# Value times gate and its remainder moved from GpSimd to VectorE in the feed-forward stage

## The chip, the core and the metric

The kernel runs on one core of a Trainium2 chip. A core has five engines with a queue each: TensorE (PE, matrix products), VectorE (DVE), ScalarE (ACT), GpSimd (POOL) and SyncE (SP), which here issues DMAs. Each queue runs in order; between engines an instruction waits for semaphores. The metric is the device time of one execution in microseconds (us).

## The reference, cut to what matters

Two transformer blocks over 256 tokens of width 1024, everything in float32. Only the feed-forward part of the first block is touched:

```
h2 = modulate(rms_norm(x, g_ffn), sh_f, sc_f)
u = einsum('bsd,df->bsf', h2, w_up)                  # 1024 -> 2 * 2816
u = causal_depthwise_conv(u, w_conv, b_conv)         # 3 taps along the tokens
u_val, u_gate = split(u, 2)
y = einsum('bsf,fd->bsd', gelu(u_gate) * u_val, w_down)   # 2816 -> 1024
x = x + gt_f * y
```

The rows `mod = silu(c) @ w_mod + b_mod` of the second block (shifts, scales and gates) are computed on VectorE in the gaps of the same stage.

## The kernel before, in words

Every product of float32 matrices is made of three TensorE products of rounded parts: `a` is `hi + lo`, `hi` is `a` rounded to float32r and `lo` the remainder, and the result is hi*hi + hi*lo + lo*hi (`triple`, L1344). Activations lie with features on the partitions and 256 tokens along the free dimension. Weights arrive in chunks of 128x2048 floats (1 MB) through four raw buffers, loaded by SP in the order `stream_order` lays down. For each chunk ScalarE casts the high part (`split` on ScalarE, L371, `w_hi`) and VectorE subtracts it (`split` on VectorE, L865, `w_lo`, called the weight remainder below); there are three slots of each, and a slot is free when TensorE has used the chunk that is three earlier (`lin_done`).

The feed-forward stage has 11 rounds, c = 0 to 10. A round has three chunks: 256 value columns, 256 gate columns and the 256 rows of `w_down` that take them in; 48 matmuls each. TensorE's order is up value(c), up gate(c), down(c-1) up to down(7); the last three down-projections stand behind round 10. Rounds 2 to 8 and 9 also carry a modulation chunk: it needs no TensorE, VectorE multiplies and sums it in four partial sums (`mod`, L832), which use a slot of `w_lo` as their waste output. In a round, by the functions' names:

- ScalarE `value_part(c)`: cast of a chunk (not in rounds 1 and 10, where `product_hi` has done it), then the first tap of the value filter out of PSUM into `cv` (`conv_first`, L560). It waits for TensorE's value block and for `g_lo_done` of round c-1, since `cv` is still read until then.
- VectorE `conv_taps(0, ...)`: the other two taps (L1034, L1039), in place; then a weight remainder.
- ScalarE `gate_part(c)` and VectorE `conv_taps(1, ...)`: the same for the gate in `cg`; then a weight remainder, in rounds 1 to 8 and 10.
- ScalarE `product_hi(c)`: gelu of `cg` (L588); behind the product, the cast of `cv` to `g_hi` (L596).
- GpSimd `product(c)`: `cv = cv * cg` behind gelu (L336), and behind the cast `g_lo = cv - g_hi` (L339).
- TensorE `down(c)` waits for `g_lo_done` and for its weights.

`cv`, `cg` and the pair `g_hi`/`g_lo` are one buffer each (round 9's pair lies in `h_hi`/`h_lo`). VectorE also has, ahead of round 10's value taps and behind its gate taps, two pieces of a norm for the next stage (`norm`, L899 and L905), into the first of which the weight remainder `ffn_up(10) + 2` is set (`chunk=`). After the last round VectorE reads the result out of PSUM bank by bank (L1074), and TensorE sums squares of it (L1601) between the last blocks of the last down-projection.

## Time and profile before

| | |
|---|---|
| median of 3 runs | 795.64 us (795.53 to 795.8) |
| the profiled execution | 795.57 us |
| its span | 793.8 us, granted clock 0.99 |
| PE busy | 751.9 us (95%) |
| DVE busy | 649.1 us (82%) |
| ACT busy | 387.9 us (49%) |
| POOL busy | 46.2 us (6%), 31 instructions |
| feed-forward stage | about 241 to 435 us |

The times in the rows further down count from the span's start. A matmul is shown with its whole latency (0.28 us), while the next one starts 0.12 us later, so a wait of TensorE under 0.2 us does not appear as idle time; the distance between two starts shows it. On VectorE and ScalarE too an instruction may start a little before the last one has ended, and the distance from start to start is what one takes of the queue. In a row of the timeline the bracket behind it is the idle time ahead of it and what ended it.

### The profile page before, as it was taken

Reading aid. Unit: us, or ns where it says so; the run is one execution under the profiler, and the core shown is the slowest. Engines: PE = TensorE matmul, PEld = TensorE weight load, DVE = VectorE, ACT = ScalarE, POOL = GpSimd, SP = SyncE. Lnnn points to the kernel's source line nnn. Section 1 sums busy time; section 2 is a strip of 40 time slices with the busy share of each in tenths; the row PEclk is TensorE's granted clock in tenths of the full one; section 3 lists DMA queues with packets and bytes.
Section 4 is the critical chain, followed back from the end, with each engine's and each line's share of the span. In section 5 each row is a group of like instructions: output and inputs, shape, how many; then the busy total and the mean of one; then the engine's idle time right before and its main releaser. Section 6 shows DMA issues by size and latency. Waiting matters only on the chain.

```text
span 793.8 us, 13124 instructions
## 1 busy us (share of the span) xinstructions
PE 751.9 (95%) x5479; PEld 697.9 (88%) x5480; DVE 649.1 (82%) x1001; ACT 387.9 (49%) x521; POOL 46.2 (6%) x31
## 2 busy tenths in 40 slices
PE   0499999999999999999999999999999999999996
PEld 0399999999999999999999998888778899999995
DVE  3988767995897799999898779999989956987752
ACT  2355645557547654544547532322463335365742
POOL 0000000000000422223222000000000000000000
PEclk9799999999999999999999999999999999999998
DMA  9999998765563557766645241313106643563101
GB/s 347 417 352 365 368 348 311 264 223 198 206 240 136 208 212 251 273 246 247 258 175 197 91 176 53 107 55 104 54 0 235 224 148 118 225 231 118 54 1 54
DMA packets 26086, 156.58 MB, mean 197 GB/s; under 512 B 2691, under 2 KB 7084, under 8 KB 7852
## 3 DMA queue, kind: packets, MB, share of 16 engines
q1 hardware_dynamic: 21392, 148.91, 50.5%
q10 hardware_dynamic: 4636, 6.85, 2.6%
q8 instruction: 43, 0.70, 0.3%
q14 instruction: 15, 0.12, 0.0%
HBM read 154.68 MB, written 1.06 MB: 196 GB/s over the span
## 4 chain that ended last, share of the span: by engine, by line
PE 84%; DVE 9%; ACT 3%; issue 1%; ACTq 1%; POOL 1%; DVEq 0%
PE psum L1344 71%; DVE w_lo L832 4%; PE psum L1379 2%; DVE w_lo L865 2%; PE psum L1636 1%; PE psum L1810 1%; PE psum L1786 1%; ACT w_hi L371 1%; PE psum L1798 1%; PE psum L1622 1%; PE psum L1486 1%; DVE arena L1034 1%; DVE arena L1039 0%; PE psum L1601 0%; PE psum L1471 0%
## 5 line engine op out<-in xcount | busy, mean ns | idle before, releaser
L1344 PE MATMUL psum<-h_hi,w_hi 128*128 128x256 f32 (+1 forms) x1312 | 397.2, 303 | 10.2 <-DVE h_lo L905 9.2
L1344 PE MATMUL psum<-h_lo,w_hi 128*128 128x256 f32 (+1 forms) x1312 | 392.1, 299 | 0.0
L1344 PE MATMUL psum<-h_hi,w_lo 128*128 128x256 f32 (+1 forms) x1312 | 392.1, 299 | 0.0
L1344 PEld LDWEIGHTS psum<-h_hi,w_hi 128*128 128x128 f32 x1312 | 251.1, 191 | 21.8 <-issue 11.6
L1344 PEld LDWEIGHTS psum<-h_lo,w_hi 128*128 128x128 f32 x1312 | 251.5, 192 | 7.8 <-issue 0.2
L1344 PEld LDWEIGHTS psum<-h_hi,w_lo 128*128 128x128 f32 x1312 | 251.3, 192 | 7.4
L865 DVE TENSOR_TENSOR w_lo<-raw,w_hi 128x2048 fp32r<-128x2048 f32 x93 | 212.7, 2288 | 50.2 <-ACT w_hi L371 49.4
L371 ACT CAST w_hi<-raw 128x2048 fp32r<-128x2048 f32 x93 | 176.9, 1905 | 20.6 <-DMA raw<-in_w 16.3
L832 DVE SCALAR_TENSOR_TENSOR w_lo<-raw,cond 128x1024 fp32r<-128x1024 f32 x88 | 119.5, 1395 | 8.3 <-PE psum L1344 7.5
L832 DVE SCALAR_TENSOR_TENSOR w_lo<-raw,arena 128x1024 fp32r<-128x1024 f32 x48 | 56.8, 1221 | 0.8
L336 POOL TENSOR_TENSOR arena<-arena 128x512 f32<-128x512 f32 x11 | 26.1, 2370 | 372.9 <-ACT arena L588 372.9
L1344 PE MATMUL psum<-g_hi,w_hi 128*128 128x256 f32 x160 | 45.7, 286 | 1.7 <-POOL g_lo L339 0.9
L1090 DVE SCALAR_TENSOR_TENSOR arena<-att,vec,arena 128x256 f32<-128x256 f32 x116 | 47.0, 479 | 0.1
L1344 PE MATMUL psum<-g_lo,w_hi 128*128 128x256 f32 x160 | 45.3, 283 | 0.0
L1344 PE MATMUL psum<-g_hi,w_lo 128*128 128x256 f32 x160 | 45.3, 283 | 0.0
L560 ACT ACTIVATE arena<-psum,vec 128x256 f32<-128x256 f32 x44 | 22.4, 561 | 37.3 <-PE psum L1344 34.2
L388 ACT ACTIVATE att<-xs 128x256 f32<-128x256 f32 x32 | 12.4, 412 | 46.5 <-DVE xs L1197 24.1
L1344 PEld LDWEIGHTS psum<-g_hi,w_hi 128*128 128x128 f32 x160 | 30.6, 191 | 2.1 <-issue 1.1
L405 ACT ACTIVATE h_hi<-att,modv 128x256 fp32r<-128x256 f32 x48 | 23.0, 506 | 16.4 <-DVE att L899 16.4
L1344 PEld LDWEIGHTS psum<-g_lo,w_hi 128*128 128x128 f32 x160 | 30.6, 191 | 0.0
L1344 PEld LDWEIGHTS psum<-g_hi,w_lo 128*128 128x128 f32 x160 | 30.6, 191 | 0.0
L899 DVE SCALAR_TENSOR_TENSOR att<-xs,coef,rstd 128x256 f32<-128x256 f32 x40 | 20.4, 534 | 11.3 <-ACT rstd L398 11.1
(214 smaller groups left out, 783.7 us busy)
## 6 DMA issues: line engine op xcount, KB each, us to landing
raw<-in_w SPq DMA_DIRECT2D x141, 1024.0 KB, 4.9
xs<-in_xs ACTq DMA_DIRECT2D x2, 1024.0 KB, 12.0
consts<-diff ACTq DMA_DIRECT2D x8, 128.0 KB, 5.5
cond<-in_cond ACTq DMA_DIRECT2D x1, 1024.0 KB, 6.4
out<-xs SPq DMA_DIRECT2D x4, 256.0 KB, 2.4
arena<-in_cond ACTq DMA_DIRECT2D x1, 512.0 KB, 6.8
consts<-in_c ACTq DMA_DIRECT2D x1, 512.0 KB, 3.4
arena<-in_c ACTq DMA_DIRECT2D x1, 448.0 KB, 3.2
```

The costliest lines, as they stand in the source:

```text
L336: nc.gpsimd.tensor_tensor(cv, cv, cg, ALU.mult).then_inc(sem("ffn_mult"), 1)
L371: nc.scalar.copy(w_hi[:, slot, :], raw[:, rslot, :]).then_inc(sem("hi_done"), 1)
L388: nc.scalar.activation(square_tmp(name)[:, k, :], xs[:, k, s * T:(s + 1) * T], ACT.Square).then_inc(sem(f"sq_{name}"), 1)
L405: nc.scalar.activation(h_hi[:, k, s * T:(s + 1) * T], norm_tmp[:, k, :], ACT.Identity, bias=shift_col(sh, k, v), scale=1.0).then_inc(sem(" ...
L560: nc.scalar.activation(dst[:, t, :], (src or bank[which])[:, t * T:(t + 1) * T], ACT.Identity, bias=col("b_conv", tile), scale=col("w_conv ...
L832: last = nc.vector.scalar_tensor_tensor(w_lo[:, slot, D * t:D * (t + 1)], raw[:, rslot, D * t:D * (t + 1)], 1.0, c, ALU.mult, ALU.mult, ac ...
L865: nc.vector.tensor_tensor(w_lo[:, slot, :], raw[:, rslot, :], w_hi[:, slot, :].bitcast(F32), ALU.subtract).then_inc(sem("lo_done"), 1)
L899: nc.vector.scalar_tensor_tensor(norm_tmp[:, k, :], xs[:, k, s * T:(s + 1) * T], coef[:, at + k:at + k + 1], rstd_of, ALU.mult, ALU.mult). ...
L1034: me.mark(nc.vector.scalar_tensor_tensor(dst[:, t, 1:T], src[:, t * T:(t + 1) * T - 1], col("w_conv", 44 + tile), dst[:, t, 1:T], ALU.mult ...
L1090: nc.vector.scalar_tensor_tensor(out, src, weight, acc, ALU.mult, ALU.add).then_inc(sem("conv_tap"), 1)
L1344: last = mm(out, w[a], x[b], start=start and n == 0, stop=stop and n == 2, skip_group_check=skip)
L1379: last = mm(bank[2 + s][:, s * T:(s + 1) * T], ones, square_tmp(name)[:, k, :], start=(k == 0), stop=(k == KT - 1))
```

## The change

GpSimd's `product` is gone; GpSimd keeps two groups of memsets. VectorE gets the same two operations as two functions, `product(c)` and `product_lo(c)`, and they are called at fixed places: the product at the end of round c, behind the weight remainder that follows the gate's taps; its remainder at the start of round c+1, behind the modulation chunk and the weight remainder there. Around rounds 9 and 10 they are set in by hand: the remainder of round 9 inside the first piece of the norm, the product and remainder of round 10 inside the last. ScalarE's and TensorE's instructions and the order of the DMAs are the same; they wait for the same semaphores.

```
-            def product(c):
-                pool.wait_ge(sem("gelu_done"), c + 1)
-                pool.wait_ge(sem("value_conv"), c + 1)
-                nc.gpsimd.tensor_tensor(cv, cv, cg, ALU.mult).then_inc(sem("ffn_mult"), 1)
-                pool.wait_ge(sem("g_hi_done"), c + 1)
-                hi, lo = ffn_g(c)
-                nc.gpsimd.tensor_tensor(lo, cv, hi.bitcast(F32), ALU.subtract).then_inc(sem("g_lo_done"), 1)
-            for c in range(FF_STEPS):
-                product(c)
...
-            def norm(name, coefs_before, rstd_of=None, ks=range(KT), chunk=None):
+            def norm(name, coefs_before, rstd_of=None, ks=range(KT), between=None):
...
-                    if i == len(ks) and chunk is not None:
-                        split(chunk)
+                    if i == len(ks) and between:
+                        between()
...
+            def product(c):
+                dve.wait_ge(sem("gelu_done"), c + 1)
+                dve.wait_ge(sem("value_conv"), c + 1)
+                nc.vector.tensor_tensor(cv, cv, cg, ALU.mult).then_inc(sem("ffn_mult"), 1)
+            def product_lo(c):
+                dve.wait_ge(sem("g_hi_done"), c + 1)
+                hi, lo = ffn_g(c)
+                nc.vector.tensor_tensor(lo, cv, hi.bitcast(F32), ALU.subtract).then_inc(sem("g_lo_done"), 1)
+            def last_split_of_values():
+                split(ffn_up(FF_STEPS - 1) + 2)
+                product_lo(FF_STEPS - 2)
+            def last_product():
+                product(FF_STEPS - 1)
+                split(ffn_down(FF_STEPS - 3) + 2)
+                product_lo(FF_STEPS - 1)
...
-                    norm("even_ctx", 4, ks=(4, 5), chunk=ffn_up(c) + 2)
+                    norm("even_ctx", 4, ks=(4, 5), between=last_split_of_values)
                 else:
                     split(ffn_up(c) + 2)
+                    if c:
+                        product_lo(c - 1)
                 conv_taps(0, cv, c, bank[2] if c == 0 else None)
                 split(ffn_up(c) + 3)
                 conv_taps(1, cg, c)
-                if 0 < c < FF_STEPS - 2 or c == FF_STEPS - 1:
-                    split(ffn_down(c - 1 if c < FF_STEPS - 2 else c - 2) + 2)
-            norm("even_ctx", 4, ks=(6, 7))
+                if 0 < c < FF_STEPS - 2:
+                    split(ffn_down(c - 1) + 2)
+                if c < FF_STEPS - 1:
+                    product(c)
+            norm("even_ctx", 4, ks=(6, 7), between=last_product)
```

VectorE's queue from the end of round 1 into round 2, before: weight remainder, the four partial sums of the modulation chunk, weight remainder, value taps.

```order
L865 TENSOR_TENSOR w_lo<-raw,w_hi 128x2048 [waits hi_done]
L832 SCALAR_TENSOR_TENSOR w_lo,modv<-raw,cond 128x1024 [waits mod_done,lin_done,arrived1]
L832 SCALAR_TENSOR_TENSOR w_lo,modv<-raw,cond 128x1024
L832 SCALAR_TENSOR_TENSOR w_lo,modv<-raw,cond 128x1024 [waits dve_steps]
L832 SCALAR_TENSOR_TENSOR w_lo,modv<-raw,cond 128x1024
L865 TENSOR_TENSOR w_lo<-raw,w_hi 128x2048 [waits hi_done,mod_done]
L1034 SCALAR_TENSOR_TENSOR arena<-psum,vec,arena 128x255 [waits tap2]
```

The same place now (the file's lines have moved by 11 there: L854 is the weight remainder, L821 the partial sums, L1023 the taps).

```order
L854 TENSOR_TENSOR w_lo<-raw,w_hi 128x2048 [waits hi_done]
L1038 TENSOR_TENSOR arena<-arena 128x512 [waits value_conv,gelu_done]
L821 SCALAR_TENSOR_TENSOR w_lo,modv<-raw,cond 128x1024 [waits mod_done,lin_done,arrived1]
L821 SCALAR_TENSOR_TENSOR w_lo,modv<-raw,cond 128x1024
L821 SCALAR_TENSOR_TENSOR w_lo,modv<-raw,cond 128x1024 [waits dve_steps]
L821 SCALAR_TENSOR_TENSOR w_lo,modv<-raw,cond 128x1024
L854 TENSOR_TENSOR w_lo<-raw,w_hi 128x2048 [waits hi_done,mod_done]
L1044 TENSOR_TENSOR g_lo<-arena,g_hi 128x512 [waits g_hi_done]
L1023 SCALAR_TENSOR_TENSOR arena<-psum,vec,arena 128x255 [waits tap2]
```

The product (L1038) stands ahead of the modulation chunk and its remainder (L1044) behind the weight remainder, directly ahead of the taps.

VectorE behind the gate taps of round 10, before: weight remainder, two norm steps, their two remainders, weight remainder.

```order
L1039 SCALAR_TENSOR_TENSOR arena<-psum,vec,arena 128x254
L865 TENSOR_TENSOR w_lo<-raw,w_hi 128x2048 [waits hi_done]
L899 SCALAR_TENSOR_TENSOR att<-xs,coef,rstd 128x256 [waits coef_ready,rstd_ready]
L899 SCALAR_TENSOR_TENSOR att<-xs,coef,rstd 128x256
L905 SCALAR_TENSOR_TENSOR h_lo<-att,modv,h_hi 128x256 [waits norm_hi] x2
L865 TENSOR_TENSOR w_lo<-raw,w_hi 128x2048 [waits hi_done]
```

And now, where L888 is the norm step and L894 its remainder.

```order
L1028 SCALAR_TENSOR_TENSOR arena<-psum,vec,arena 128x254
L888 SCALAR_TENSOR_TENSOR att<-xs,coef,rstd 128x256 [waits coef_ready,rstd_ready]
L888 SCALAR_TENSOR_TENSOR att<-xs,coef,rstd 128x256
L1038 TENSOR_TENSOR arena<-arena 128x512 [waits value_conv,gelu_done]
L854 TENSOR_TENSOR w_lo<-raw,w_hi 128x2048 [waits hi_done]
L1044 TENSOR_TENSOR g_lo<-arena,g_hi 128x512 [waits g_hi_done]
L894 SCALAR_TENSOR_TENSOR h_lo<-att,modv,h_hi 128x256 [waits norm_hi] x2
L854 TENSOR_TENSOR w_lo<-raw,w_hi 128x2048 [waits hi_done]
```

The weight remainder of the last chunk has moved behind the norm steps and the product, and the product's remainder behind it.

## Rows read from the trace of the kernel before

Columns of a timeline: start in us, length in us, engine, line, operation, out<-in with shapes, count; in brackets the idle time ahead of it and what ended it.

**Rows 1.** Page, part 1: busy time, share and instructions of each engine.
```profile
PE 751.9 (95%) x5479; PEld 697.9 (88%) x5480; DVE 649.1 (82%) x1001; ACT 387.9 (49%) x521; POOL 46.2 (6%) x31
```

**Rows 2.** Stretch of the stage's steady part: length, busy time, granted clock, DMA.
```profile
282.00:398.00 116.00, 115.50 (x962) 115.51 (x963) 111.45 (x126) 57.82 (x61) 28.62 (x14) 1.00 0.68 253
```

**Rows 3.** Timeline of ScalarE, rounds 7 to 9: start, length, line, tiles, [idle before].
```profile
373.10 0.63 ACT L588 ACTIVATE arena<-arena 128x512 f32<-128x512 f32 x1 [1.10 <-DVE arena L1039]
376.45 0.62 ACT L596 CAST g_hi<-arena 128x512 fp32r<-128x512 f32 x1 [2.72 <-POOL arena L336]
376.98 1.90 ACT L371 CAST w_hi<-raw 128x2048 fp32r<-128x2048 f32 x1
380.71 1.02 ACT L560 ACTIVATE arena<-psum,vec 128x256 f32<-128x256 f32 x2 [1.83 <-PE psum L1344]
...
397.99 1.02 ACT L560 ACTIVATE arena<-psum,vec 128x256 f32<-128x256 f32 x2 [2.10 <-PE psum L1344]
```

**Rows 4.** Timeline of VectorE, rounds 7 and 8.
```profile
358.18 2.31 DVE L832 SCALAR_TENSOR_TENSOR w_lo<-raw,cond 128x1024 fp32r<-128x1024 f32 x1
...
375.18 2.32 DVE L832 SCALAR_TENSOR_TENSOR w_lo<-raw,cond 128x1024 fp32r<-128x1024 f32 x1
...
382.20 2.29 DVE L865 TENSOR_TENSOR w_lo<-raw,w_hi 128x2048 fp32r<-128x2048 f32 x1
```

**Rows 5.** Timeline of TensorE at its three waits in the stage.
```profile
281.46 0.28 PE L1344 MATMUL psum<-h_hi,w_lo 128*128 128x256 f32 x1
282.50 0.39 PE L1344 MATMUL psum<-g_hi,w_hi 128*128 128x256 f32 x1 [0.75 <-DVE w_lo L865]
...
409.19 0.28 PE L1344 MATMUL psum<-h_hi,w_lo 128*128 128x256 f32 x1
409.59 0.39 PE L1344 MATMUL psum<-h_hi,w_hi 128*128 128x256 f32 x1
...
426.85 0.28 PE L1344 MATMUL psum<-h_hi,w_lo 128*128 128x256 f32 x1
428.05 0.36 PE L1344 MATMUL psum<-g_hi,w_hi 128*128 128x256 f32 x1 [0.91 <-POOL g_lo L339]
```

**Rows 6.** Timeline of VectorE in round 9, GpSimd empty.
```profile
400.74 1.22 DVE L832 SCALAR_TENSOR_TENSOR w_lo<-raw,cond 128x1024 fp32r<-128x1024 f32 x1
...
405.56 2.29 DVE L865 TENSOR_TENSOR w_lo<-raw,w_hi 128x2048 fp32r<-128x2048 f32 x1
407.76 0.87 DVE L1034 SCALAR_TENSOR_TENSOR arena<-psum,vec,arena 128x255 f32<-128x255 f32 x2
```

**Rows 7.** Timeline of GpSimd, the remainder of round 7.
```profile
377.15 1.52 POOL L339 TENSOR_TENSOR g_lo<-arena,g_hi 128x512 fp32r<-128x512 f32 x1 [0.73 <-ACT g_hi L596]
```

**Rows 8.** Group of VectorE's operation of 128x512, later stage: busy, mean ns, idle.
```profile
L1134 DVE TENSOR_TENSOR arena<-arena 128x512 f32<-128x512 f32 x4 | 2.6, 684 | 0.0
```

**Rows 9.** Timeline of VectorE in that later stage, two in a row.
```profile
497.06 1.29 DVE L1134 TENSOR_TENSOR arena<-arena 128x512 f32<-128x512 f32 x2
```

**Rows 10.** Timeline, round 10: ScalarE's filter start, VectorE's next weight remainder.
```profile
415.70 1.02 ACT L560 ACTIVATE arena<-psum,vec 128x256 f32<-128x256 f32 x2 [2.38 <-PE psum L1344]
...
418.55 2.29 DVE L865 TENSOR_TENSOR w_lo<-raw,w_hi 128x2048 fp32r<-128x2048 f32 x1
```

**Rows 11.** Timeline, rounds 0 and 1: VectorE's remainder, ScalarE's first filter start.
```profile
260.64 2.29 DVE L865 TENSOR_TENSOR w_lo<-raw,w_hi 128x2048 fp32r<-128x2048 f32 x1 [2.49 <-ACT w_hi L371]
...
264.18 1.02 ACT L560 ACTIVATE arena<-psum,vec 128x256 f32<-128x256 f32 x2 [3.05 <-POOL g_lo L339]
```

**Rows 12.** Timeline of VectorE behind round 9; norm steps with and without GpSimd.
```profile
409.45 0.40 DVE L883 TENSOR_TENSOR modv<-modv,vec 128x8 f32<-128x8 f32 x2
...
410.25 2.01 DVE L899 SCALAR_TENSOR_TENSOR att<-xs,coef,rstd 128x256 f32<-128x256 f32 x2
...
438.94 1.28 DVE L899 SCALAR_TENSOR_TENSOR att<-xs,coef,arena 128x256 f32<-128x256 f32 x3 [0.47 <-ACT arena L619]
```

**Rows 13.** Timeline of TensorE in the stage's last down-projection, the sums of squares.
```profile
432.84 1.10 PE L1601 MATMUL psum<-arena 128*128 128x256 f32 x4 [0.25 <-ACT arena L388]
```

## Prediction

> **What bounds the kernel now.** I read the page first: TensorE is busy for 751.9 us of a span of 793.8 us [rows 1]. Then a table by stretches around the feed-forward stage: in its steady part, 282 to 398 us, TensorE is busy for 115.50 of 116.00 us at a granted clock of 1.00, and VectorE for 111.45 us too [rows 2]. So two engines look full, and the question is which one sets the pace. The timeline answers it. ScalarE's first step on a finished value block, which ends a wait for TensorE there, comes at 380.71 and 397.99 us: 17.28 us a round [rows 3]. VectorE's rounds start at 358.18 and 375.18 us: 17.00 us [rows 4]. TensorE is the slower and is not idle there: 962 matmuls in 115.50 us, 0.120 us each, 144 of them a round [rows 2]. What the stage can gain at most is therefore TensorE's few waits, read as steps between neighbouring matmul starts, less the usual 0.12 and with 0.10 for the slow restart behind each: 281.46 to 282.50 (1.02 us, for a weight remainder of VectorE), 409.19 to 409.59 (0.38, for the gate's filter), 426.85 to 428.05 (1.15, for GpSimd's remainder of the last product) [rows 5]. Together 2.55 us, 0.3% of the kernel.
>
> **What goes.** GpSimd's 22 operations (46.2 us busy with its few memsets) [rows 1]. They cost VectorE time: a partial sum of a modulation chunk takes 2.31 or 2.32 us while GpSimd works [rows 4] and 1.22 us without it; in round 9, with GpSimd empty, the block of four with their reads goes from 400.74 to 405.56, 4.82 us [rows 6], where it is 382.20-375.18 = 7.02 us in round 8 [rows 4]. So 2.20 us of VectorE's round go.
>
> **What comes.** Two VectorE operations of 128x512 a round. The same form between two SBUF operands takes 684 ns [rows 8], and two in a row 1.29 us [rows 9], so one takes 0.605 us of the queue and 0.69 us until another engine sees it. VectorE's work per round becomes 17.00-2.20+1.21 = 16.0 us, less than TensorE's 17.28. But these sums are not the pace, because a ring closes that was open before. ScalarE may start the value filter of round c+1 only behind the remainder of round c, and that remainder now stands on VectorE behind the product, the modulation chunk and a weight remainder. Before, it was done at 377.15+1.52 = 378.67 us, ahead of TensorE's block (380.71) [rows 3, 7]. Now, with a(c) the start of ScalarE's value filter of round c, each step from a row:
> - ScalarE's two filter starts, its cast, VectorE's weight remainder: VectorE starts that remainder 418.55-415.70 = 2.85 us after a [rows 10];
> - that remainder 2.20 (405.56 to 407.76) [rows 6]; gate filter 407.76 to 409.45, 1.69 [rows 6, 12]; the next weight remainder 2.20;
> - product 0.61 (gelu, 0.63 us [rows 3], is hidden by the remainder before it); modulation 4.82 [rows 6]; remainder 2.20 (ScalarE's cast of it, 1.90 us, is hidden by the 4.82);
> - product remainder and hand to ScalarE 0.69+0.03.
>
> Sum 17.29, say 17.30 us. It holds no TensorE step, so it runs at its own pace, and it is TensorE's pace to within 0.02 us. VectorE is idle in it for some 1.1 us, the 1.02 us of ScalarE's filter start [rows 10] and two handoffs.
>
> **Where the ring starts, and what TensorE sees.** In round 0 the product now runs at once, beside ScalarE's cast, and the remainder follows the weight remainder begun at 260.64: 260.64+2.20+0.69+0.03 = 263.56, where a(1) was 264.18 (released by GpSimd) [rows 11]. So a(2) = 263.56+17.30 = 280.86, and the weight remainder that TensorE waited for is done 0.69 us before this, at about 280.2. TensorE comes at 281.58, so its wait of 1.02 us goes: **-1.02**. From here TensorE's schedule is 1.02 earlier: the down-projections want the product's remainder at 281.58+17.28n and get it at 280.86+17.30n, 0.7 us ahead at first, 0.6 at the last. No wait in the steady part.
>
> **Round 9 gives it back.** a(8) = 263.56+7x17.30 = 384.66. Round 9 has no modulation chunk before its first weight remainder, but ScalarE's cast for it stands behind its cast of the product: 2.85+2.20+1.69+2.20 = 8.94, product until ScalarE sees it 0.72, cast of the product 0.53 and weight cast 1.90+0.03 (376.45, 376.98) [rows 3], remainder 2.20, product remainder 0.72: 15.04 us. a(9) = 399.70. Before it was 397.99, when TensorE's block was there [rows 3]. So round 9 starts 1.71 us later, and what follows is word for word as before: taps, modulation, remainder, gate taps, on which TensorE waits at 409.59 [rows 3, 5, 6]. Its gate block of round 10 starts at 411.30: **+1.71 against before**, although it was ready at 408.3.
>
> **Round 10.** Gate filter of round 9 done at 411.25; gelu until 411.9; product to 412.55; biases and coefficients 0.80 (409.45 to 410.25) [rows 12]; two norm steps, which take 2.01 with GpSimd beside them, 0.80 (three without it take 1.28, 0.40 from start to start) [rows 12]; weight remainder 2.20; product remainder: a(10) = 417.1 instead of 415.70. From there 2.85+2.20+1.69, norm steps 0.80, product 0.61, weight remainder 2.20, product remainder 0.69: 428.1 us. TensorE runs its 144 matmuls from 411.30 and arrives at 428.7, after both. So its wait of 1.15 us goes, and the last down-projection starts at 428.7 instead of 428.05: +0.65. Before, TensorE then stood again, from 428.05+0.07+36x0.12 = 432.4 to 432.84, for ScalarE's squares, which stand behind its own casts and table load [rows 13]. Those hardly move: the last cast needs a slot that TensorE frees at 428.8, about when ScalarE comes to it. TensorE comes at 428.7+4.3 = 433.0, finds two squares ready, and so 0.4 of the 0.65 is taken up there. **Net: +0.2 us** at the end of the stage, and everything behind it shifts by that.
>
> The profiled execution took 795.57 us (span 793.8 and 1.8 around it); the median of three runs is 795.64, so +0.07. Forecast 795.57+0.2+0.07, about **795.9 us**.
>
> A rule that speaks for a longer ring. The Trainium skill, "VectorE: DVE Perf Modes", § The DRAIN you can't avoid, says that after every VectorE operation the next does not start until the pipe is empty, a gap between starts. Taken so, an added product would fill its whole 0.684 us, not 0.605, and the ring would be 0.08 longer, some 0.6 us by round 9. The trace disagrees: two of 684 ns end within 1.29 us, so the second starts before the first has ended [rows 8, 9]. I keep 0.605.
>
> **Unknown costs, bounded.** The product waits for ScalarE's gelu and the remainder for ScalarE's cast on an engine whose other waits are of the same kind, 0.02 to 0.05 us in the rows; between nothing and 0.1 us a round for all handoffs I have not seen together, so -0.1 to +0.1 on a ring of 17.30. Seven rounds make that -0.7 to +0.7, and it passes in full to the gate block of round 10. Floor: if TensorE found nothing to wait for in rounds 9 and 10, -1.0-0.4-1.15 = -2.55.
>
> **Rivals.**
> - *Cover is enough (faster).* VectorE's work of 16.0 us is what counts, the ring never binds, and all three waits of TensorE go: 795.64-2.55 = 793.1 us. For it speaks that VectorE gets 1 us freer a round; against it, that a(9) would have to be 1.7+0.4 us earlier, a ring of 17.0, and every step of the ring has a row.
> - *The ring is longer than TensorE's round (slower).* Beyond 17.40 TensorE waits for the product's remainder in the steady part as well, and round 9 takes each round's excess too. At 17.55 the last down-projection comes 1.75 later than forecast: 797.6 us. From about 17.5 it leaves the bound of no change. For it speaks that the ring has no slack and several handoffs; against it, that the known ones are all 0.02 to 0.05 us.
> - *The slow partial sums are not GpSimd's doing.* Then 2.20 us stays in the ring, 19.5 us, and TensorE waits about 2.2 us in each of seven rounds: 811 us. Against it: round 9, where all four fit in 4.82 us [rows 6].
>
> **Chances.** A measurement of this kernel can tell about 0.2%, 1.6 us, from no change. Forecast and its neighbourhood (794.6 to 797.0) 0.80; cover is enough 0.07; long ring 0.12; third rival 0.01. Of the second 0.02 and of the third 0.03 still lie within 1.6 us (a ring a little short of 17.0, or one under 17.5): faster 0.05, within 0.85, slower 0.09+0.01 = 0.10. The range, 794.3 to 797.4, takes the ring's 0.1 a round both ways and part of the two rivals.
>
> **What would show it.** Partial sums all at 1.22 us in the stage; the two added operations near 0.68 us; ScalarE's value filter released by VectorE's product remainder, 17.3 us apart, from 263.6 to 384.7; VectorE idle about 1.1 us a round before its taps; no matmul gap at 281.5; one of about 2.9 us before 411.3; none before the last down-projection. Wrong would be a ring away from 17.30 by over 0.1, or a TensorE wait between 282 and 398.

## The result, and the profile after

The changed kernel takes 797.77 us, the median of 14 executions (796.24 to 798.57); the kernel before, on the same chip, 795.75 us (795.53 to 796.28). The ratio is 1.0022, with a 95% interval of 1.0014 to 1.0030: slower by 0.2%. The forecast was 795.9 us with a range up to 797.4, so it was wrong, by 1.9 us. The prediction had given slower a chance of 0.10.

One thing is needed to read the numbers. The 14 executions fall into two groups: three lie at 796.24 to 796.37 us, eleven at 797.60 to 798.57 us, with nothing between. The profiled one (797.76 us, span 796.0) is of the upper group. What parts the two groups is what the experiments are about.

The page of the kernel after, part 1, against [rows 1]:

```profile
PE 753.1 (95%) x5480; PEld 699.5 (88%) x5480; DVE 644.3 (81%) x1023; ACT 387.4 (49%) x521; POOL 1.1 (0%) x9
```

TensorE has the same matmuls and is busy 1.2 us longer. VectorE has 22 operations more and is busy 4.8 us less; GpSimd is left with its memsets. The window of the steady part, against [rows 2]:

```profile
282.00:398.00 116.00, 116.00 (x969) 115.98 (x968) 105.44 (x138) 59.28 (x62) 0.00 (x0) 1.00 0.66 245
```

The matmuls now fill all 116.00 us: no wait of TensorE is left between 282 and 398 us. VectorE's busy time has gone from 111.45 to 105.44 us. VectorE's timeline of one whole round, against [rows 4]:

```profile
280.34 0.69 DVE L1044 TENSOR_TENSOR g_lo<-arena,g_hi 128x512 fp32r<-128x512 f32 x1
282.17 0.87 DVE L1023 SCALAR_TENSOR_TENSOR arena<-psum,vec,arena 128x255 f32<-128x255 f32 x2 [1.15 <-ACT arena L549]
...
283.97 2.29 DVE L854 TENSOR_TENSOR w_lo<-raw,w_hi 128x2048 fp32r<-128x2048 f32 x1
286.18 0.87 DVE L1023 SCALAR_TENSOR_TENSOR arena<-psum,vec,arena 128x255 f32<-128x255 f32 x2
...
287.87 2.28 DVE L854 TENSOR_TENSOR w_lo<-raw,w_hi 128x2048 fp32r<-128x2048 f32 x1
290.07 0.68 DVE L1038 TENSOR_TENSOR arena<-arena 128x512 f32<-128x512 f32 x1
290.67 1.22 DVE L821 SCALAR_TENSOR_TENSOR w_lo<-raw,cond 128x1024 fp32r<-128x1024 f32 x1
...
295.49 2.29 DVE L854 TENSOR_TENSOR w_lo<-raw,w_hi 128x2048 fp32r<-128x2048 f32 x1
297.70 0.68 DVE L1044 TENSOR_TENSOR g_lo<-arena,g_hi 128x512 fp32r<-128x512 f32 x1
```

The partial sum at 290.67 takes 1.22 us, where it took 2.32 us beside GpSimd. The product (290.07) and its remainder (280.34, 297.70) take 0.68 and 0.69 us, and the bracket at 282.17 shows VectorE idle for 1.15 us before its taps. ScalarE's value filters, against [rows 3, 11], are now all released by VectorE's product remainder:

```profile
263.75 1.02 ACT L549 ACTIVATE arena<-psum,vec 128x256 f32<-128x256 f32 x2 [2.51 <-DVE g_lo L1044]
...
281.12 1.02 ACT L549 ACTIVATE arena<-psum,vec 128x256 f32<-128x256 f32 x2 [5.26 <-DVE g_lo L1044]
...
298.48 1.02 ACT L549 ACTIVATE arena<-psum,vec 128x256 f32<-128x256 f32 x2 [5.25 <-DVE g_lo L1044]
...
385.27 1.02 ACT L549 ACTIVATE arena<-psum,vec 128x256 f32<-128x256 f32 x2 [5.26 <-DVE g_lo L1044]
...
400.37 1.02 ACT L549 ACTIVATE arena<-psum,vec 128x256 f32<-128x256 f32 x2 [3.02 <-DVE g_lo L1044]
```

One round is 298.48-281.12 = 17.36 us, and it ends in ScalarE's bracket, not in TensorE's block as before. So the ring that the prediction describes exists. The last row, a(9) = 400.37, is 2.38 us later than the 397.99 of before.

TensorE at its waits, and at the start of the last down-projection, against [rows 5]:

```profile
402.54 0.28 PE L1360 MATMUL psum<-h_hi,w_lo 128*128 128x256 f32 x1
403.26 0.39 PE L1360 MATMUL psum<-h_hi,w_hi 128*128 128x256 f32 x1 [0.44 <-DVE arena L1028]
...
408.99 0.28 PE L1360 MATMUL psum<-h_hi,w_lo 128*128 128x256 f32 x1
411.97 0.39 PE L1360 MATMUL psum<-h_hi,w_hi 128*128 128x256 f32 x1 [2.70 <-DVE arena L1028]
412.20 0.28 PE L1360 MATMUL psum<-h_lo,w_hi 128*128 128x256 f32 x1
...
413.70 0.41 PE L1360 MATMUL psum<-h_lo,w_hi 128*128 128x256 f32 x1
413.91 0.41 PE L1360 MATMUL psum<-h_hi,w_lo 128*128 128x256 f32 x1
...
430.82 0.28 PE L1360 MATMUL psum<-g_hi,w_hi 128*128 128x256 f32 x1
```

The wait at 281.5 us is gone. The one for the gate's filter has grown to 411.97-408.99 = 2.98 us from start to start, 2.70 of it idle. The last down-projection starts at 430.82 without a wait, where it started at 428.05. A short wait at 402.54 for the value's filter (0.44 us) was not forecast.

Now look at 413.70 and 413.91: the matmul takes 0.41 instead of 0.28 us and the next starts 0.21 later instead of 0.12. Seven windows of 1 us show the same stretch (busy time and count of TensorE's matmuls and weight loads, VectorE, ScalarE, GpSimd, then the granted clock and the DMA):

```profile
411.00:412.00 1.00, 0.03 (x1) 0.03 (x1) 0.88 (x3) 0.05 (x1) 0.00 (x0) 1.00 1.04 434
412.00:413.00 1.00, 1.00 (x8) 1.00 (x9) 0.39 (x1) 1.00 (x2) 0.00 (x0) 1.00 1.04 434
413.00:414.00 1.00, 1.00 (x9) 1.00 (x8) 0.84 (x5) 1.00 (x1) 0.00 (x0) 0.75 0.96 401
414.00:415.00 1.00, 1.00 (x7) 1.00 (x7) 0.98 (x3) 1.00 (x3) 0.00 (x0) 0.50 0.45 188
415.00:416.00 1.00, 1.00 (x6) 1.00 (x6) 1.00 (x1) 0.70 (x2) 0.00 (x0) 0.50 0.00 0
416.00:417.00 1.00, 1.00 (x7) 1.00 (x6) 1.00 (x1) 0.00 (x0) 0.00 (x0) 0.54 0.00 0
417.00:418.00 1.00, 1.00 (x11) 1.00 (x10) 1.00 (x3) 0.20 (x1) 0.00 (x0) 1.00 0.00 0
```

The granted clock is 1.00 while TensorE stands and for the first microsecond of its work, then 0.75, 0.50, 0.50 and 0.54, and then 1.00 again. 0.50 is the 1.2 GHz level. The counts (a matmul that reaches into two windows counts in both) are 6 or 7 there and 11 at the full clock in the last row, although TensorE is busy all the time; the starts per microsecond fall from 7 to 4 or 5 and then rise to 9. Of the matmuls from 411.97 to 430.82, 16 have a step of 0.213 us instead of 0.120: 16x0.093 = 1.49 us. At the end of the stage TensorE finds the first squares ready:

```profile
435.14 1.02 PE L1617 MATMUL psum<-arena 128*128 128x256 f32 x4
435.82 0.47 PE L1360 MATMUL psum<-g_hi,w_hi 128*128 128x256 f32 x1
```

Before, the squares started at 432.84 [rows 13], behind an idle wait, and the next down-projection matmul in the same timeline at 433.59. So this point is 435.82-433.59 = 2.23 us later, and so is the span (796.0 against 793.8). Of the 2.77 us at the last down-projection 0.54 was taken up here.

In sum, against before: +2.38 at the gate block of round 10, 411.97-409.59 (1.71 forecast; the 1.02 gained at 281.5 is in it), +1.49 for the slow matmuls, -1.15 for the wait ahead of the last down-projection, -0.54 at the squares: 2.18 of the 2.2 us. Against the forecast, +0.67 and +1.49.

### The profile page after: what moved, and what is told of

The parts are those of the page before. It is cut to its first block, busy times and chain, and to the rows that moved or that the text cites. A ratio compares the mean times of both kernels' runs of the same rounds, so it can differ in the third digit from the quotient of the medians.

```text
span 796.0 us, 13123 instructions
## 1 busy us (share of the span) xinstructions
PE 753.1 (95%) x5480; PEld 699.5 (88%) x5480; DVE 644.3 (81%) x1023; ACT 387.4 (49%) x521; POOL 1.1 (0%) x9
## 4 chain that ended last, share of the span: by engine, by line
PE 88%; DVE 7%; ACT 2%; ACTq 1%; issue 1%; DMA 1%; DVEq 0%
PE psum L1360 75%; DVE w_lo L821 2%; PE psum L1395 2%; DVE w_lo L854 1%; PE psum L1652 1%; PE psum L1826 1%; PE psum L1802 1%; DMA raw<-in_w 1%; PE psum L1814 1%; PE psum L1638 1%; PE psum L1502 1%; ACT w_hi L360 0%; PE psum L1487 0%; ACTq L347 0%; PE psum L1451 0%
## 5 line engine op out<-in xcount | busy, mean ns | idle before, releaser
L854 DVE TENSOR_TENSOR w_lo<-raw,w_hi 128x2048 fp32r<-128x2048 f32 x93 | 212.7, 2288 | 47.7 <-ACT w_hi L360 46.8
L821 DVE SCALAR_TENSOR_TENSOR w_lo<-raw,cond 128x1024 fp32r<-128x1024 f32 x88 | 104.1, 1220 | 8.3 <-PE psum L1360 7.5
L821 DVE SCALAR_TENSOR_TENSOR w_lo<-raw,arena 128x1024 fp32r<-128x1024 f32 x48 | 56.8, 1220 | 0.7
L1395 PE MATMUL psum<-att,c 128*128 128x256 f32 x64 | 18.1, 431 | 11.9 <-ACT att L377 11.9
L1023 DVE SCALAR_TENSOR_TENSOR arena<-psum,vec,arena 128x255 f32<-128x255 f32 x44 | 19.1, 476 | 10.7 <-ACT arena L549 10.7
```

What stands on the lines that cost most here:

```text
L821: last = nc.vector.scalar_tensor_tensor(w_lo[:, slot, D * t:D * (t + 1)], raw[:, rslot, D * t:D * (t + 1)], 1.0, c, ALU.mult, ALU.mult, ac ...
L854: nc.vector.tensor_tensor(w_lo[:, slot, :], raw[:, rslot, :], w_hi[:, slot, :].bitcast(F32), ALU.subtract).then_inc(sem("lo_done"), 1)
L1023: me.mark(nc.vector.scalar_tensor_tensor(dst[:, t, 1:T], src[:, t * T:(t + 1) * T - 1], col("w_conv", 44 + tile), dst[:, t, 1:T], ALU.mult ...
L1395: last = mm(bank[2 + s][:, s * T:(s + 1) * T], ones, square_tmp(name)[:, k, :], start=(k == 0), stop=(k == KT - 1))
```

## The experiments

**The theories.** A stand is a stretch in which TensorE waits without a matmul. A: the ring of 17.36 us and round 9 make TensorE stand 2.9 us, which costs little by itself, and the clock falls after that stand; the fall makes most of the loss. B: something in the new order (VectorE's or ScalarE's traffic around 413 to 417 us) slows the matmuls, and the stand has no part in it. C: the ring alone costs the 2 us, and the slow matmuls are hidden behind the wait for the last product's remainder. D, added later: the fall comes from the two stands together, the short one at 402.5 and the long one. Every kernel below was timed beside the kernel before. All changes are to the changed kernel unless "before" is said. None leaves a part of the computation out; the fillers add matmuls or products whose result nobody reads.

### Keeping TensorE at work during the stand (a_fill, a_fill5)

Twelve matmuls of zeros ahead of the wait for the gate's filter, in round 10 alone; a_fill5 has five.

```diff
+                if c == FF_STEPS - 1:
+                    pe.wait_ge(sem("rstd_ready"), 3)
+                    for _ in range(12):
+                        mm(bank[3][:, :], zeros[:, 0:P], zeros[:, :], start=True, stop=True, skip_group_check=True)
                 pe.wait_ge(sem("gate_conv"), c)
```

> The changed kernel with 12 matmuls of zeros (128x512, bf16, into a PSUM bank nobody reads) in TensorE's queue right ahead of its wait for the gate filter of round 9, so that it works through most of the 2.9 us instead of standing. Nothing else differs. Theory A (the stand lowers the granted clock, and 16 matmuls behind it run at 0.21 us instead of 0.12): the slow matmuls go, the gate block still starts near 412.0, the last down-projection starts about 1.4 us earlier, and the time falls by 1.2 to 1.5 us, to about 796.4. Theory B (something else beside those matmuls slows them: VectorE's or ScalarE's work or a transfer at 413.5 to 417 us): they stay, 797.8. Theory C (the ring alone costs the 2 us, the slow matmuls are hidden behind the last product's remainder): they may go, but the time stays at 797.8.

> The changed kernel with five matmuls of zeros at the start of the stand instead of twelve: TensorE stands for 1.9 us instead of 2.9 or 0.4. With twelve the clock fell in 1 of 11 executions, and in the kernel whose stand is 1.8 us (remainder ahead in round 9) in 1 of 11. Expected if a stand of under 2 us leaves the clock alone: as with twelve, median 796.4. If any stand there brings it down as often as one of 2.9 us: 797.7.

Measured: a_fill 796.41 us (796.21 to 797.10, 11 executions), ratio 1.0007 [0.9998, 1.0016]; a_fill5 796.25 us (796.16 to 796.99, 11), ratio 1.0007 [0.9998, 1.0016]. The upper group is gone: 0 of 11 in a_fill5, at most the one at 797.10 in a_fill. TensorE's timeline of a_fill at the stand (the 12 added matmuls lie where the dots are), and its window around it:

```profile
409.57 0.28 PE L1360 MATMUL psum<-h_hi,w_lo 128*128 128x256 f32 x1
...
412.57 0.38 PE L1360 MATMUL psum<-h_hi,w_hi 128*128 128x256 f32 x1
```

```profile
408.00:420.00 12.00, 11.82 (x89) 10.17 (x89) 10.69 (x20) 5.35 (x8) 0.00 (x0) 1.00 0.55 198
```

The gate block starts even later (412.57 instead of 411.97, since twelve matmuls are more than the stand holds), and yet the kernel is 1.4 us faster, at a granted clock of 1.00 through the whole window. With five, TensorE still stands idle for 1.60 us, and the upper group is gone all the same; c_after, the changed kernel timed beside a_fill5 on the same chip, has six of eleven executions in it. The last down-projection starts at 429.93 and at 429.28 instead of 430.82. Nothing on VectorE or ScalarE was changed, so theory B falls; the time went down with the slow matmuls, so C falls too, for this kernel. The changed kernel without the fall takes about 796.3 us, which is also where its own lower group lies.

### The stand alone, in the kernel before (b_delay4, c_delay4, b_delay6)

Four idle products on VectorE ahead of the gate taps of round 9, each waiting for the one before it, 2.78 us in all, 0.69 each and not the 0.6 of the expectation (b_delay6 has six; c_delay4 is b_delay4 again):

```diff
                 split(ffn_up(c) + 3)
+                if c == FF_STEPS - 2:
+                    for n in range(4):
+                        if n:
+                            dve.wait_ge(sem("spare_done"), n)
+                        nc.vector.tensor_tensor(mix[:, 0:512], cond[:, 0, 0:512], cond[:, 1, 0:512],
+                                                ALU.mult).then_inc(sem("spare_done"), 1)
                 conv_taps(1, cg, c)
```

> The kernel before, product on GpSimd, with four idle VectorE multiplications of 128x512 (2.4 us, result unread) ahead of the gate taps of round 9. TensorE's wait ahead of the gate block of round 10 grows from 0.3 to 2.7 us. Theory A: some 16 matmuls at 0.21 us follow it though nothing of the change is in this kernel, and the time is 2.2 to 2.6 us above before, 798.1. Theory B: no slow matmuls, the last down-projection waits as before for the last remainder, which is 2.4 us later: 797.5 to 798.0. The matmuls tell them apart, not the time.

> The kernel before with four idle VectorE multiplications in round 9 again: a stand of TensorE of 3.1 us, as long as in the changed kernel. It fell in 1 of 5. If the length of the stand alone sets how often the clock falls, this one and the changed kernel fall equally often on one chip (above 799.9 here). If they differ again, 1 in 5 against 4 in 5, something else in what TensorE does around the stand counts as well.

> The kernel before with six idle VectorE multiplications (3.6 us) ahead of the gate taps of round 9 instead of four: TensorE waits some 4.0 us before the gate block of round 10 instead of 3.1. With four, four runs of five lay at 798.4 to 798.8 us and one at 800.1, where the clock had fallen. If the length of the stand decides, most runs show the fall here: 799.7 without it, 801.2 with it, median near 801. If it is a matter of when the stand falls, not of its length alone, the share of such runs need not grow: median near 799.8.

Measured: with four 798.75 us (798.39 to 800.11, 5), ratio 1.0035 [1.0023, 1.0048], and once more 798.53 us (798.39 to 799.85, 5), ratio 1.0038 [1.0026, 1.0051]; with six 800.63 us (799.77 to 803.13, 6), ratio 1.0062 [1.0049, 1.0074]. Timeline of TensorE with four, and the windows 408 to 420 us with four and with six:

```profile
409.68 0.28 PE L1350 MATMUL psum<-h_hi,w_lo 128*128 128x256 f32 x1
412.87 0.39 PE L1350 MATMUL psum<-h_hi,w_hi 128*128 128x256 f32 x1 [2.90 <-DVE arena L1039]
...
430.12 0.28 PE L1350 MATMUL psum<-h_hi,w_lo 128*128 128x256 f32 x1
431.30 0.36 PE L1350 MATMUL psum<-g_hi,w_hi 128*128 128x256 f32 x1 [0.91 <-POOL g_lo L339]
```

```profile
408.00:420.00 12.00, 9.10 (x76) 8.89 (x75) 11.25 (x18) 4.79 (x8) 4.31 (x2) 1.00 0.48 185
```

```profile
408.00:420.00 12.00, 7.64 (x47) 7.44 (x46) 11.61 (x19) 3.75 (x5) 3.59 (x2) 0.72 0.39 164
```

With four, TensorE stands 2.90 us idle, a little longer than in the changed kernel, and in the profiled execution the clock stays at 1.00: the 2.9 us are paid, and no more. I had expected a fall there, so this one went against theory A as I first held it. The time is above both expectations, since the wait grew by 3.19-0.40 = 2.79 us and not by 2.4. The profiled execution of c_delay4 shows the same: 2.90 us idle, no slow matmul.

With six, the stand is 414.70-410.06 = 4.64 us, 4.36 of it idle, and the granted clock of the window is 0.72: 20 matmuls behind the stand have a step of 0.213 us, +1.86 us. This kernel has GpSimd's product and none of the changed order, so a stand alone can bring the fall. Five of its six executions have a mean clock of 0.988 or lower; that is a weaker sign (one of them, 803.13 us, has 0.940, which is far more than such a fall).

How often the clock falls with four can't be read from the times. In this kernel TensorE waits 431.30-430.12 = 1.18 us for GpSimd's last remainder and then for the squares, as in the kernel before, and a fall hides there, as theory C has it. With six it shows: the gate block starts 414.70-412.87 = 1.83 us later than with four, the squares 438.41-436.09 = 2.32 us later, so only some 0.5 of the 1.86 us reach the time. A fall of 16 matmuls with four would cost next to nothing. Of the ten executions with four, seven lie at 798.39 to 798.82 and three at 799.73 to 800.11, with mean clocks of 0.987 or 0.988; two of the fastest (798.39 and 798.45) have 0.989. By mean clock it is three to five of ten, and why three are 1.3 us slower isn't shown. So the second measurement, which was to compare how often the clock falls here and in the changed kernel, doesn't settle it.

### The changed kernel again, and the short stand (c_after, a_valfill)

c_after is the changed kernel word for word. a_valfill puts three of the zero matmuls ahead of the short wait of round 10:

```diff
+                if c == FF_STEPS - 1:
+                    pe.wait_ge(sem("rstd_ready"), 3)
+                    for _ in range(3):
+                        mm(bank[3][:, :], zeros[:, 0:P], zeros[:, :], start=True, stop=True, skip_group_check=True)
                 if c > 1:
                     pe.wait_ge(sem("value_conv"), c)
```

> The changed kernel again, beside the next two on one chip, to compare how often the clock falls behind the stand of 2.9 us. It fell in 11 of 14 executions (797.6 to 798.6 us against 796.2 to 796.4). If that is a property of the stand: most executions here at 797.6 or above. If it was one of the chip or of the hour: as few as in the delayed kernel below.

> The changed kernel with three matmuls of zeros ahead of TensorE's other, short wait in round 10 (0.6 us, before the value block, for the value filter of round 9), the long wait of 2.9 us left as it is. If the short wait helps to bring the clock down at the long one, most runs take 796.3 us, as those of the changed kernel without slow matmuls. If the long wait alone decides it, most take 797.7 as before.

Measured: c_after 797.84 us (796.16 to 799.27, 11), ratio 1.0019 [1.0010, 1.0027], five of them at 796.16 to 796.36 and six at 797.84 to 799.27. Together with the first measurement 17 of 25 executions are in the upper group; a fall is read from the group and the mean clock there (0.986 to 0.989 against 0.990 or 0.991), and from the windows only in the two profiled ones, which both have 16 slow matmuls. The upper group reaches from 797.60 to 799.27 us, 1.3 to 3.0 above the lower; no trace shows its slower members. a_valfill 798.15 us (796.33 to 799.32, 10), ratio 1.0027 [1.0018, 1.0036]: eight of ten in the upper group. Filling the short stand does not take the fall away, so theory D falls. The long one decides. The profiled execution of a_valfill (796.50 us) happens to be of the lower group. It has the same long stand. Its TensorE there, then the windows 408 to 420 us of the changed kernel and of a_valfill:

```profile
409.22 0.28 PE L1360 MATMUL psum<-h_hi,w_lo 128*128 128x256 f32 x1
412.20 0.39 PE L1360 MATMUL psum<-h_hi,w_hi 128*128 128x256 f32 x1 [2.70 <-DVE arena L1028]
```

```profile
408.00:420.00 12.00, 9.30 (x65) 9.09 (x64) 10.70 (x19) 5.95 (x8) 0.00 (x0) 0.86 0.60 221
```

```profile
408.00:420.00 12.00, 9.30 (x78) 9.10 (x77) 10.65 (x20) 5.73 (x8) 0.00 (x0) 1.00 0.59 212
```

The same 2.70 us idle and the same busy time, with 65 matmuls at a clock of 0.86 and 78 at 1.00: after one and the same stand the clock fell in one execution and not in the other. The last down-projection starts at 429.58 instead of 430.82, although the gate block started 0.23 us later: that is the fall's 1.47 us again.

### Opening the ring (a_early, a_lo9)

a_early puts the product's remainder ahead of the weight remainder in every round, a_lo9 in round 9 only:

```diff
-                    split(ffn_up(c) + 2)
-                    if c:
-                        product_lo(c - 1)
+                    mods = mods_before(ffn_up(c) + 2)
+                    for m in mods:
+                        mod_static(m, ffn_up(c) + 2)
+                    if c:
+                        product_lo(c - 1)
+                    split(ffn_up(c) + 2, done=len(mods))
```

```diff
+                    if c == FF_STEPS - 2:
+                        product_lo(c - 1)
                     split(ffn_up(c) + 2)
-                    if c:
+                    if 0 < c < FF_STEPS - 2:
                         product_lo(c - 1)
```

> The changed kernel with the product's remainder behind the modulation chunk but ahead of the weight remainder in every round. If the ring is what paces VectorE and ScalarE, it loses the 2.2 us of the weight remainder and TensorE paces all rounds: ScalarE's filter start of round 8 near 380 instead of 385.3, a wait of TensorE ahead of the gate block of round 10 under 0.5 us, no slow matmuls, no wait before the last down-projection: 793.3 us. If VectorE's own work is what matters, nothing changes: 797.8.

> The changed kernel with the product's remainder of round 8 ahead of the weight remainder in round 9 alone (it is ready when ScalarE has cast the product, at 395.5, and waited until 399.6). ScalarE's filter start of round 9 then waits for its own cast only: 397.4 instead of 400.4; VectorE's taps come at 399.6 instead of 401.4, and so does everything up to the gate filter, so TensorE's gate block of round 10 starts at 410.1 instead of 412.0 and waits 1.6 us instead of 2.9. Theory A: if the clock does not fall at such a wait, the last down-projection starts at 427.6, the kernel takes 795.0 us, below before; if it falls all the same, 796.2. Theory B and C: 1.8 us less than the changed kernel, 796.0.

Measured: a_early 793.19 us (793.03 to 793.67, 5), ratio 0.9965 [0.9952, 0.9977]; a_lo9 794.62 us (794.34 to 795.27, 11), ratio 0.9983 [0.9974, 0.9992]. ScalarE's value filters of rounds 8 and 9 and TensorE at the gate block, in a_early:

```profile
380.04 1.02 ACT L549 ACTIVATE arena<-psum,vec 128x256 f32<-128x256 f32 x2 [3.27 <-PE psum L1363]
...
397.32 1.02 ACT L549 ACTIVATE arena<-psum,vec 128x256 f32<-128x256 f32 x2 [3.28 <-PE psum L1363]
...
408.52 0.28 PE L1363 MATMUL psum<-h_hi,w_lo 128*128 128x256 f32 x1
408.93 0.38 PE L1363 MATMUL psum<-h_hi,w_hi 128*128 128x256 f32 x1
```

ScalarE is released by TensorE's block again, every 17.28 us, as before the change, and the stand is down to 0.41 us from start to start. The last down-projection starts at 426.29 us, 1.76 ahead of before. This version beats both kernels. The same in a_lo9:

```profile
397.75 1.02 ACT L549 ACTIVATE arena<-psum,vec 128x256 f32<-128x256 f32 x2
...
408.80 0.28 PE L1362 MATMUL psum<-h_hi,w_lo 128*128 128x256 f32 x1
410.65 0.38 PE L1362 MATMUL psum<-h_hi,w_hi 128*128 128x256 f32 x1 [1.57 <-DVE arena L1028]
```

Here the ring still runs at its own pace up to round 8, but round 9's filter starts at 397.75 instead of 400.37, TensorE stands 1.57 us idle, and one of eleven executions shows a lower clock (795.27 us, mean 0.988). The time was expected at 795.0 us by theory A, without a fall, or 796.2 with one, and at 796.0 by B and C. Its last down-projection starts at 428.01, where before has 428.05 [rows 5]; the wait at the squares that goes makes its profiled execution 0.6 us shorter (794.95 against 795.57), and the medians lie 1.2 us apart (794.62 against 795.80 beside it). Both kernels change nothing but the place of the remainder, so the ring and round 9 are what made the stand.

### One of the two operations back on GpSimd (a_lopool, a_prodpool)

Each adds a loop to GpSimd's program and drops the same operation from VectorE's. First a_lopool, the remainder on GpSimd, then a_prodpool, the product on GpSimd:

```diff
+            for c in range(FF_STEPS):
+                pool.wait_ge(sem("g_hi_done"), c + 1)
+                hi, lo = ffn_g(c)
+                nc.gpsimd.tensor_tensor(lo, cv, hi.bitcast(F32), ALU.subtract).then_inc(sem("g_lo_done"), 1)
```

```diff
+            for c in range(FF_STEPS):
+                pool.wait_ge(sem("gelu_done"), c + 1)
+                pool.wait_ge(sem("value_conv"), c + 1)
+                nc.gpsimd.tensor_tensor(cv, cv, cg, ALU.mult).then_inc(sem("ffn_mult"), 1)
```

> Half of the change: the product on VectorE where the change puts it, the remainder on GpSimd as before. The remainder no longer stands behind the modulation chunk and a weight remainder, so the ring is open: ScalarE's filter starts follow TensorE, 17.28 us apart (round 8 near 380, not 385.3). One partial sum a round stays slow. The ring theory: no wait of TensorE up to round 9, one of about 0.3 us before the gate block of round 10, no slow matmuls, 793.5 to 794.5 us. If it is VectorE's added work that costs the time (its work per round is 16.5 us here, 16.0 in the changed kernel), it is slower than the changed kernel or equal: 797.8 or more.

> The other half: the product on GpSimd as before, the remainder on VectorE where the change puts it. The ring stays closed and grows: VectorE's 0.61 us of the product go, one partial sum of the next chunk takes 1.09 us more beside GpSimd: 17.36-0.61+1.09 = 17.84 us a round, 0.56 more than TensorE's. The ring theory: TensorE waits for the product's remainder in the later rounds of the steady part, 0.5 us each, the start of round 9 is some 3.4 us later than in the changed kernel (400.4), and the time is 800 to 801.5 us. If VectorE's work is what matters (0.61 less, 1.09 more), it is 797.8 to 798.5.

Measured: a_lopool 794.62 us (794.17 to 798.08, 11), ratio 0.9989 [0.9980, 0.9997]; a_prodpool 802.31 us (802.05 to 802.87, 4), ratio 1.0082 [1.0069, 1.0095]. With the remainder off VectorE's queue the ring is open: ScalarE's filter of round 8 is released by TensorE, and the last down-projection pays a short wait for GpSimd. The median is 0.1 us above the range expected; that wait was not in it. One of the eleven executions (798.08 us, mean clock 0.989) lies 3.0 us above the next; no trace shows why.

```profile
380.24 1.02 ACT L554 ACTIVATE arena<-psum,vec 128x256 f32<-128x256 f32 x2 [3.28 <-PE psum L1361]
...
426.44 0.28 PE L1361 MATMUL psum<-h_hi,w_lo 128*128 128x256 f32 x1
427.22 0.36 PE L1361 MATMUL psum<-g_hi,w_hi 128*128 128x256 f32 x1 [0.51 <-POOL g_lo L336]
```

With the product on GpSimd, slower and beside the partial sums, the ring is longer instead. ScalarE's filters of rounds 3 and 4 and TensorE at the down-projection just behind the second:

```profile
299.34 1.02 ACT L554 ACTIVATE arena<-psum,vec 128x256 f32<-128x256 f32 x2 [5.21 <-DVE g_lo L1049]
...
317.20 1.02 ACT L554 ACTIVATE arena<-psum,vec 128x256 f32<-128x256 f32 x2 [5.21 <-DVE g_lo L1049]
...
316.62 0.28 PE L1362 MATMUL psum<-h_hi,w_lo 128*128 128x256 f32 x1
317.25 0.36 PE L1362 MATMUL psum<-g_hi,w_hi 128*128 128x256 f32 x1 [0.35 <-DVE g_lo L1049]
```

The round is 317.20-299.34 = 17.86 us, as expected to 0.02, and TensorE waits for the product's remainder in each steady round (317.25-316.62 = 0.63 from start to start). The total was expected at 800 to 801.5 us and missed by 0.8: a(9) came 3.9 us later than in the changed kernel, not 3.4: 3.34 of it by round 8, and round 9 itself took 404.28-388.61 = 15.67 us instead of 15.10, with the product of round 8 still 2.61 us long on GpSimd. In the profiled execution TensorE also stands 2.70 us idle ahead of the gate block, and 16 slow matmuls follow. This is the prediction's second rival, made on purpose.

## Why the prediction was wrong

The step that failed is this one: "TensorE runs its 144 matmuls from 411.30 and arrives at 428.7". It prices each matmul at 0.120 us, the step of the steady part [rows 2], right behind the longest stand of the stage. The prediction had itself put that stand at 2.9 us ("one of about 2.9 us before 411.3") and counted only the waiting. The profiled execution paid 16 of the matmuls at 0.213 us, +1.49 us, and by their times so did about two executions in three. The fillers show that the stand is the cause, and b_delay6 shows it without the change. None of the signs that the prediction names for itself looks at the matmuls behind the stand: the signs of being right came true, neither sign of being wrong appeared, and the time was outside the range all the same.

Point by point:

- *What goes.* Right. The partial sums take 1.22 us and TensorE's wait at 281.5 us is gone.
- *What comes.* Right: 0.68 and 0.69 us, and the start-to-start distance of two neighbours is 290.67-290.07 = 0.60, as priced.
- *The ring.* Right in kind, 17.36 us where 17.30 was forecast. The piece that was too small is the hand from VectorE's remainder to ScalarE: 280.34+0.69 = 281.03, and ScalarE starts at 281.12, 0.09 us instead of 0.03. It lay within the bounds given (0.1 a round). The other pieces are as priced, to 0.01. a(1) was 263.75 where 263.56 was forecast, a(8) 385.27, not 384.66; a(9) 400.37, not 399.70; the gate block 411.97, not 411.30: +0.67, of which 0.19 at a(1), 0.42 in the seven rounds and 0.06 in round 9.
- *No wait in the steady part, none before the last down-projection.* Right. The ring is longer than TensorE's round by 0.08 us, and the lead of 0.7 us that it starts with outlasts the seven rounds.
- *Round 10.* The last down-projection is TensorE's pace, as forecast. 428.7+0.67+1.49 = 430.86, and 430.82 was measured.
- *The squares.* Right: 0.4 forecast, 0.54 us measured.
- *Sum.* With the +0.67, less the 0.14 more at the squares, the forecast would have been 796.4; the executions without the fall lie at 796.2 to 796.4, and a_fill5 at 796.25. So without the fall the kernel is some 0.5 us slower than before, where 0.2 was forecast, and the rest is the clock.

On the rivals: "cover is enough" needed another order to come true, and that its price fits (793.1 against the 793.19 of a_early) is in part luck: in a_early the wait ahead of the gate block is still there (0.41 us from start to start), and a wait at the squares goes that the price had left out. "The ring is longer" came true only by 0.06 us a round and never reached the 17.40 from which TensorE would have waited; its price of 797.6 us lies near the 797.77 measured by chance, since it was worked out for a ring of 17.55. The rival on the other side that decided, a stand long enough for the clock to fall, was missing, and so the range ended at 797.4.

The Trainium skill, "TensorE: Matmul & The Clock Gate", Part 1, says that TensorE's clock is gated down by lack of activity and let up again by activity, and that the number of matmuls which run at the low level differs from run to run of one kernel. The traces here agree on the first: 1.00 up to the stand, 0.50 behind it, 1.00 again once TensorE has worked for a while. On the second, the two traces of the changed kernel have 16 slow matmuls each, and only its two groups of times say that the number differs. The price, 0.213 us a matmul instead of 0.120, is from the trace.

**What stays open.** Why the fall comes in one execution and not in the next. The stand of 2.70 us was followed by slow matmuls in the profiled executions of the changed kernel (both) and of a_prodpool and not in that of a_valfill; 2.90 us were followed by none in either profiled one of the delayed kernel. Six traces can't tell whether the changed order makes the fall likelier, and the delayed kernel's times don't count its falls. A mean clock is a weak sign besides, since it takes in other stretches that differ from one profiled execution to the next (30 to 40 us: 0.53 to 0.68; 785 to 790 us: 0.72 to 1.00): in a_prodpool the two executions at 0.988 (802.05 and 802.17 us) are faster than the two at 0.992, and among the executions of the kernel before, with no long stand there, two have 0.989 (796.64 and 797.01 us).

## What to carry to other kernels

An operation moved off a slow engine can close a ring through queues that was open; add up the ring's pieces, and put the handed-over piece ahead of the long operation that does not need it (a_early: the same operations in another order, 4.6 us faster than the changed kernel). When a change makes TensorE stand for one long stretch instead of several short ones, price the matmuls behind the stand at both clock levels, and look for a later wait that would hide the difference (1.49 us paid in full in the changed kernel, 0.5 of 1.86 in b_delay6). A kernel whose executions form two groups has something that happens or doesn't: split the times before comparing medians.

## What the runs showed of the hardware

- After 2.70 us idle the times and mean clocks say that TensorE's granted clock fell in 17 of 25 executions of the changed kernel and in eight of ten of a_valfill; after 1.60 us in none of eleven (a_fill5), after 1.57 us in at most one of eleven (a_lo9). The traces show the fall after 2.70 us in three executions of four, after 2.90 us in none of two, after 4.36 us in the one there is. It shows in the windows from 413 to 417 us, when TensorE is back at work since 411.97, and costs 16 matmuls of 0.213 us instead of 0.120, 1.5 us.
- A fall need not reach the time: with 20 slow matmuls, +1.86 us, b_delay6 is 0.5 us later, since TensorE waits less for GpSimd's last remainder and the squares.
- Zero matmuls into an unused bank keep the clock up: in a_fill the kernel is faster although TensorE reaches its work 0.60 us later.
- The hand from a VectorE operation to ScalarE's filter took 0.09 us in the ring, where the prediction had put 0.03, from other pairs.
- VectorE operations of 128x512 follow each other 0.60 us from start to start (290.07 to 290.67) and 0.69 us when each waits for the one before it (b_delay4: four in 2.78 us).
